# Recurrence units of a delta-rule mixer: two 64x64 chunks per tile on the partition halves, eight tap buffers

## The reference, cut to what matters

```
def _wkv7(r, decay, k, v, a_vec, b_vec):
    def step(S, inp):
        r_t, w_t, k_t, v_t, a_t, b_t = inp
        sa = jnp.einsum("bhvk,bhk->bhv", S, a_t)
        S = S * w_t[:, :, None, :] + sa[..., None] * b_t[:, :, None, :] + v_t[..., None] * k_t[:, :, None, :]
        y = jnp.einsum("bhvk,bhk->bhv", S, r_t)
        return S, y
...
    y = _wkv7(r_h, decay.reshape(B, T, H, N), k_h, v_h, -kk, kk * a_h)
...
    c = u[..., :D_CONV] * jax.nn.sigmoid(u[..., D_CONV:])
    c = _causal_dwconv(c, cconv_w, cconv_b)
    c = jax.nn.silu(_layer_norm(c, cln_g, cln_b))
```

## Time and profile before

| what | value |
|---|---|
| median of 3 executions | 1712.69 us (1710.89 to 1716.49) |
| the profiled execution | 1717.92 us |
| its span in the profile | 1716.1 us |
| TensorE busy over the span | 1651.0 us, 96% |
| VectorE, ScalarE, GpSimd busy | 1008.8, 734.9, 958.2 us |
| mean granted TensorE clock | 0.981 of full speed |

### The profile page before, as it was taken

How to read it: one execution, slowest core, us unless ns; L and a number is a source line. 1 busy time by engine, 2 the same in 40 slices (tenths; PEclk the granted TensorE clock), 3 DMA queues, 4 the chain that set the end, 5 groups by cost and what they waited for, 6 DMA issues and landing times.

```text
span 1716.1 us, 26361 instructions
## 1 busy us (share of the span) xinstructions
PE 1651.0 (96%) x10600; PEld 1353.4 (79%) x10600; DVE 1008.8 (59%) x1271; ACT 734.9 (43%) x1250; POOL 958.2 (56%) x758
## 2 busy tenths in 40 slices
PE   8999999899999999998999999999989999999887
PEld 7677999867888888887886777767877888888775
DVE  4699566574755553004446667665665666666565
ACT  4553787433322221005325565654144444444562
POOL 3454799783999999995462203217535444444062
PEclk9999999999999999999999999999989999999998
DMA  5221000542222224332111000003131111111211
GB/s 198 74 78 70 2 1 1 201 147 99 95 92 92 92 96 172 121 135 78 71 50 50 1 25 25 0 1 130 53 151 49 50 50 50 50 50 50 99 50 49
DMA packets 18872, 126.40 MB, mean 74 GB/s; under 512 B 2096, under 2 KB 2352, under 8 KB 4304
## 3 DMA queue, kind: packets, MB, share of 16 engines
q1 hardware_dynamic: 18624, 124.41, 20.0%
q10 hardware_dynamic: 144, 0.52, 0.1%
HBM read 122.83 MB, written 2.10 MB: 73 GB/s over the span
## 4 chain that ended last, share of the span: by engine, by line
PE 59%; issue 16%; POOL 11%; DVE 8%; ACT 5%; DMA 0%; POOLq 0%; ACTq 0%; DVEq 0%; SPq 0%
POOL w_hi L654 8%; PE banks L1293 5%; PE banks L905 4%; PE banks L1272 4%; POOL w_lo L645 4%; PE banks L1450 4%; PE banks L1453 3%; PE banks L1451 3%; PE banks L1155 3%; PE banks L1160 3%; PE banks L1156 3%; PE banks L1505 2%; PE banks L757 2%; PE banks L758 2%; PE banks L759 2%
## 5 line engine op out<-in xcount | busy, mean ns | idle before, releaser
L654 POOL TENSOR_TENSOR w_hi<-raw,der 128x512 fp32r<-128x512 f32 x296 | 332.7, 1134 | 428.4 <-PE banks L1453 187.3
L645 POOL TENSOR_TENSOR w_lo<-raw,w_hi 128x512 fp32r<-128x512 f32 x336 | 479.4, 1439 | 67.1 <-ACT w_hi L1596 67.1
L757 PE MATMUL banks<-h_hi,w_hi 128*128 128x512 f32 x464 | 184.3, 397 | 0.3 <-DVEq L2271 0.3
L758 PE MATMUL banks<-h_lo,w_hi 128*128 128x512 f32 x464 | 180.7, 389 | 0.0
L759 PE MATMUL banks<-h_hi,w_lo 128*128 128x512 f32 x464 | 180.6, 389 | 0.0
L1450 PE MATMUL banks<-h_hi,w_hi 128*128 128x512 f32 (+1 forms) x384 | 147.1, 383 | 0.1
L1451 PE MATMUL banks<-h_lo,w_hi 128*128 128x512 f32 (+1 forms) x384 | 132.1, 359 | 0.0
L2111 ACT ACTIVATE dP<-banks,der 128x768 f32<-128x768 f32 x64 | 57.7, 902 | 161.0 <-DVE der L2920 161.0
L704 POOL TENSOR_TENSOR Of<-Of,Ls 128x768 f32<-128x768 f32 x8 | 14.7, 1833 | 186.7 <-DVE Ls L2722 186.7
L1453 PE MATMUL banks<-h_hi,w_lo 128*128 128x512 f32 (+1 forms) x384 | 117.1, 359 | 0.0
L757 PEld LDWEIGHTS banks<-h_hi,w_hi 128*128 128x128 f32 x464 | 87.1, 188 | 25.6 <-issue 7.5
(11 more groups left out here) (507 smaller groups left out, 4089.1 us busy)
## 6 DMA issues: line engine op xcount, KB each, us to landing
raw<-in_stream SPq DMA_DIRECT2D x84, 1024.0 KB, 4.8
ada_raw<-in_ada_w SPq DMA_DIRECT2D x18, 1024.0 KB, 7.0
raw<-in_ada_w SPq DMA_DIRECT2D x4, 1024.0 KB, 4.8
xT<-in_x_t SPq DMA_DIRECT2D x2, 1024.0 KB, 6.1
xT<-in_x_t SPq DMA_DIRECT2D x1, 2048.0 KB, 8.2
ada_end<-in_ada_w SPq DMA_DIRECT2D x2, 1024.0 KB, 6.0
out_t<-z SPq DMA_DIRECT2D x8, 256.0 KB, 2.1
ctxT<-in_ctx_t SPq DMA_DIRECT2D x1, 1024.0 KB, 7.0
```

Of the source, the lines that this page charges most:

```text
L645: return pool.tensor_tensor(lo[:, h, part(i), :], raw_tiles(half)[:, part(i), :], hi[:, h, part(i), :], ALU.subtract)
L654: pool.tensor_tensor(hi[:, h, part(i), :], raw_tiles(half)[:, part(i), :], one, ALU.mult).then_inc(hi_done, 1)
L757: pe.matmul(banks[b][:, :], hi, tile(rhs_hi, k), start=(at_k == 0), stop=False)
L758: pe.matmul(banks[b][:, :], hi, tile(rhs_lo, k), start=False, stop=False)
```

## The change

A unit's 128-token tile becomes two chunks of 64, on the two halves of the partitions. Every tile Di, DiT, Lt, Gt, Mt, RKt and RBt is 128 x 4 x 64 in place of 128 x 4 x 128, and each 128x128 product becomes two products of 64x64 by 64x64, whose places in the PE array alternate. A step of one head is eight matmuls in place of four. The copies, masks, placements and transposes are over 256 columns in place of 512. Mt has a tile of its own, DiT has two in turn (c even or odd), and the orders of PE, ACT and DVE are written out by hand: the next pair's LT and identity come ahead of this pair's Q5, W and U. Three PSUM banks serve a head: one for G (and W), one for LT and P, one for all the rest, so that MT, RB, RK, MV, Y0, Q5 and U of a head wait for one another's readers. Y0's copy and W's scaling are one instruction for both heads. The scaling of eR stands by itself (`eR`, once a pair). The taps stay on ScalarE and GpSimd with eight buffers in place of four, and all stand behind G1 to G5 and U (5, 4, 4, 4, 3, 4 in each pair); none stand behind the identity, MV or Y0.

```
-    tap_out = [glu_s[:, 0, :], glu_s[:, 1, :]] + [reg(f"tap_out{i}", [P, T], 141 + 2 * i)[:, :] for i in range(2)]
+    tap_out = [glu_s[:, 0, :], glu_s[:, 1, :]] + [reg(f"tap_out{i}", [P, T], kb)[:, :] for i, kb in enumerate((141, 143, 46))] + \
+        [at(f"tap_out{3 + i}", [P, T], F32, tmp_at + 2 * i * KB)[:, :] for i in range(3)]
...
+    PE_ORDER, ACT_ORDER, DVE_ORDER = [(0, "LT")], [(0, "ID"), (0, "LT")], [(0, "DT0", 0), (0, "D0", 0), (0, "DT0", 1), (0, "D0", 1)]
+    for c in range(CT):
+        last = c == CT - 1
+        PE_ORDER += [(c, s) for s in ("MT", "G1", "RB", "P1", "RK", "G2", "P2", "MV", "G3", "P3", "Y0", "G4", "P4", "G5")]
+        PE_ORDER += ([] if last else [(c + 1, "LT")]) + [(c, s) for s in ("Q5", "W", "U")]
+        ACT_ORDER += [(c, s) for s in ("G1", "G2", "MV", "G3", "Y0", "G4")] + ([] if last else [(c + 1, "ID")])
+        ACT_ORDER += [(c, "G5")] + ([] if last else [(c + 1, "LT")]) + [(c, "U")]
+        DVE_ORDER += [(c, "MT", 0), (c, "MT", 1), (c, "P1", 0), (c, "T1", 0), (c, "P1", 1), (c, "T1", 1), (c, "RB", 0), (c, "RB", 1),
+                      (c, "P2", 0), (c, "T2", 0), (c, "P2", 1), (c, "T2", 1), (c, "RK", 0), (c, "RK", 1),
...
+    PROD_BANK, BACK_BANK, MIX_BANK = (0, 1), (2, 3), (4, 5)
...
+            def by_chunk(b, lhs, rhs):
+                for tt in range(4):
+                    for r in HEAD:
+                        mm = pe.matmul(b[r, CHUNK * tt:CHUNK * tt + CHUNK], lhs[r, tt, :], rhs[r, tt, :], start=True, stop=True)
+                mm.then_inc(u_pe[e], 1)
...
         def tap(i):
             t, j = ADDED[i]
-            if i >= 4:
-                act.wait_ge(conv_done, i - 3)
...
+            if i >= len(tap_out):
+                act.wait_ge(conv_done, i - len(tap_out) + 1)
...
-        TAPS_BEHIND = {"DIT": 5, "MV": 1, "Y0": 1, "G1": 3, "G2": 3, "G3": 3, "G4": 3, "G5": 3, "U": 2}
+        TAPS_BEHIND = {"G1": 5, "G2": 4, "G3": 4, "G4": 4, "G5": 3, "U": 4}
```

More of the change, by code:

```diff
@@ new lines, in by_chunk, with to_features @@
+            def by_chunk(b, lhs, rhs):
+                for tt in range(4):
+                    for r in HEAD:
+                        mm = pe.matmul(b[r, CHUNK * tt:CHUNK * tt + CHUNK], lhs[r, tt, :], rhs[r, tt, :], start=True, stop=True)
+                mm.then_inc(u_pe[e], 1)
+            def to_features(out, lhs, rhs):
+                for tt in range(4):
+                    for half, r in enumerate(HEAD):
+                        mm = pe.matmul(banks[out[half]][rows, CHUNK * tt:CHUNK * tt + CHUNK], lhs[r, tt, cols], rhs[r, tt, :], start=True, stop=True)
+                mm.then_inc(u_pe[e], 1)
@@ L919, in _ @@
+        for c, step in PE_ORDER:
+            for e in range(2):
+                unit(c, e, step)
         pe.wait_ge(silu_c, 1)
@@ L1728, in _ @@
-        next_tap = 0
-        for c in range(CT):
-            for step in ACT_STEPS:
-                for e in range(2):
-                    unit(c, e, step)
-                n_taps = TAPS_BEHIND.get(step, 0)
-                for i in range(next_tap, next_tap + n_taps):
-                    tap(i)
-                next_tap += n_taps
+                out, src = U[:, :, 64 * h:64 * h + 64], banks[MIX_BANK[e]]
+            act.activation(out, src[:, 0:256].rearrange("p (a b) -> p a b", a=4), ACT.Copy).then_inc(u_act[e], 1)
@@ new lines, in _ @@
+        TAPS_BEHIND = {"G1": 5, "G2": 4, "G3": 4, "G4": 4, "G5": 3, "U": 4}
+        next_tap = 0
+        act.wait_ge(block_done, N_IN)
+        for c, step in ACT_ORDER:
+            if step == "Y0":
+                first_y(c)
+            else:
+                for e in range(2):
+                    if step == "ID":
+                        identity(c, e)
+                    else:
+                        unit(c, e, step)
+            for i in range(next_tap, next_tap + TAPS_BEHIND.get(step, 0)):
+                tap(i)
+            next_tap += TAPS_BEHIND.get(step, 0)
@@ L2419, in unit @@
                 dve.wait_ge(u_pe[e], pe_at(c, step))
-                placed(*((Di[e], bank(1), n) if step[0] == "P" else (DiT[e], bank(2), 6 + n)))
-        for c in range(CT):
-            for step in DVE_STEPS:
-                for e in range(2):
-                    unit(c, e, step)
+                placed(*((Di[e], bank(BACK_BANK), n) if step[0] == "P" else (T_now, bank(MIX_BANK), 6 + n)))
+        for c, step, e in DVE_ORDER:
+            unit(c, e, step)
+        chain.wait()
         chain.link(dve.memset(der[:, ROOT:ROOT + 4], 0.0))
```

266 lines of the change are left out of this document (127 added, 139 removed).

## The result

The changed kernel takes **1726.99 us** (median of 10, 1720.00 to 1730.33) against 1713.89 of the kernel before on the same chip (median of 10): a ratio of 1.0072, 95% interval 1.0057 to 1.0086. It is 0.7% slower. 1705.1 was forecast, with 1699 to 1716 as the range. The profiled execution's span is 1728.5 us for 1716.1.

The account below looks back on a forecast made before the run. PE was taken to set the units' pace, GpSimd's adds close behind and next to bound. Earlier end of adds -6.6 and chunk chain -1.0 make -7.6 us: median 1712.69 becomes 1705.1, range 1699 to 1716.

Parts of the forecast that it names:

- the cost of VectorE: Units: VectorE's small operations, eR and W take 13.5 us a pair, below the adds.
- case (a): Units: GpSimd's tap adds set the pace, 30.15 us a pair; kernel at 1701 to 1709 us; chance 0.70.
- The adds' end: Units: last GpSimd tap add ends at 303.2 against 309.77, -6.6 us, with a first add at 182.6.
- the chain: Chunk chain behind the adds: between +3.0 and -5.1 us, taken as -1.0.
- The price of a record: PE in the units: a 64x64 product's record costs 0.032 us at full clock, 0.0575 at half.
- Rival (c): Units: each PE record costs 0.0575 us throughout, 39.6 us a pair; kernel slower at 1743 us; chance 0.08.
- The loop of a pair: Units: PE's work of 18.5 us plus 6.5 without work makes 25 us a pair at full clock.
- rival (b): Units: the unit loop sets the pace through clock falls and larger bubbles; kernel at 1708.5 to 1715.3 us; chance 0.14.
- Rival (e): Units: a 64x64 pair costs as much as a 128x128 product, 32 us a pair; chance within that of rival (b).
- Rival (d): Chunk chain: issue stretches vanish, half clock is short, start at its lower bound; kernel at 1699 to 1702 us; chance 0.08.
- The cold restart: Chunk chain: starts at half clock after 11 idle us; 3.5 us of it lose 1.5, 6.9 lose 3.0.
- GpSimd idle in the middle of the stage: Units: sign that the forecast is wrong, pointing to rival (b) or Rival (c) by the granted clock.

Follow-up runs that it names:

- e2: Changed kernel with the decay operand of eR's scaling read from a PSUM bank: 1709.75 us, 0.9948 of the kernel before.
- e10: Changed kernel with the decay in PSUM and 20 taps of channel block 3 moved to VectorE: 1695.41 us, 0.9886 of the kernel before.
- e8: e2 with the wait for the adds and conv_sums one chunk later (n = 2) in the chunk chain: 0.9949 of the kernel before.
- e9: e8 with the first two taps taken ahead to the first LT: 0.9937 of the kernel before.
- e13: Changed kernel, eR's scaling behind a long-met wait in pairs 0, 1, 3 and written to another tile in pair 2: 1730.13 us, a single time.
- e6: e2 with 28 added VectorE products of 8 columns, both operands in SBUF, seven a pair: 1729.82 us, a single time.
- e11: e2 with 28 added VectorE products of 512 columns, both operands in SBUF, at the places of e6: 1726.75 us, a single time.
- e3: Changed kernel with four tap buffers in place of eight: 1.0045 of the kernel before.

## Why the prediction was wrong, point by point

**The step that failed** is the cost of VectorE: "VectorE has 28 small ones, 11.8, and eR and W, each put at two small ones, 1.7: 13.5. Both lie below the adds." For all of these but eR it held (0.45, 0.43, 0.42, 0.68 us each). eR was put at the price of its size; it cost 38.7 us in all, 36 more than four times 0.65. The sum then took for granted that VectorE has more than half of the time free, and never asked which of its instructions can run beside a GpSimd add. The earlier trace rows gave a hint, the two adds beside eR at 206.69 with 2.94 us against 2.52. The forecast read this as a cost to GpSimd (0.42 us, inside the 120.60) and not as a sign that the two take turns. That they do is in the kernel before already. VectorE, then GpSimd around it:

```profile
207.64 0.86 DVE L2392 TENSOR_TENSOR eR<-eR,der 128x512 f32<-128x512 f32 x1
```

```profile
207.91 1.71 POOL L676 TENSOR_TENSOR cacc<-glu_s,cacc 128x512 f32<-128x512 f32 x1
210.93 1.27 POOL L676 TENSOR_TENSOR cacc<-tap_out,cacc 128x512 f32<-128x512 f32 x1 [1.30 <-ACT tap_out L1694]
```

eR stands at 207.64 with an add running and one filled buffer behind it. It is let in at the end of the running add, and the next add takes 1.71 us. The gap of 1.30 us comes only after both. So eR did not need a gap in the kernel before, in any of its four pairs, and what changed so that it is held in three of four is not shown. What is shown is the price of a hold: it lasts until GpSimd has nothing to do, and "GpSimd without idle" is what the forecast wanted.

The Trainium skill has the rule (SBUF — State Buffer, Who interferes with whom): a VectorE instruction with two inputs in SBUF contends with a GpSimd instruction that reads SBUF, by an exclusive lock, and one with a single SBUF input doesn't (outside of modes that take two ports). The traces agree on who contends: eR does, W and e2's eR don't. By the same section the one that issues first has the ports for its whole instruction; the other would then wait for one add, an estimated 1.3 us at most by the adds' length here. For 53 of the 56 probes, the four eR of the kernel before and the first of the changed kernel the traces agree: where there was a wait, it ended with the running add. For the others they differ: eR stood for 10 to 13.9 us, with seven to ten adds started after it.

**The mechanism behind it was right, where it could work.** The likeliest case (a), the adds set the pace, is what e2 shows once eR is out of the way: first add 182.72 (182.6), last 301.59 (303.2), the units' end on PE at 289.2 (288), `conv_sums` 8.7 us earlier than before, and 337.39 against 345.90 for the output projection, -8.5 us for a forecast of -7.6. The adds' end moved by -8.2 where -6.6 was forecast (adds of 1.230 us in place of 1.256 give -2.5, idle +0.8, the start +0.1); `conv_sums` stands closer behind them, -0.5; the chain gave +0.2 where -1.0 was taken. That the total of e2 comes so near the forecast is in part luck, as the misses of -1.6 and -0.5 make up for the +1.2 of the chain. In time e2 is 0.52% faster; the forecast was 0.44%.

**The price of a record** held: 32 in 0.96 us at full clock, 0.030 us, and 1.73 us, 0.054, at the lower level (forecast 0.032 and 0.0575). Rival (c), half clock or issue throughout, is excluded by this. One reading beside it was wrong and touches no term of the sum. The prediction set the 62 ns per matmul of the Trainium skill (TensorE: Matmul & The Clock Gate, Back-to-back issue gap) against the 32 records of a step. But the profile records each matmul twice, so a step has 16 matmuls, and 16 times 62 ns is an estimated 0.99 us. That is close to the 1.03 us of the row: the trace doesn't speak against that figure, and the 2.0 us a step and the +15 us of rival (c) that were worked out from it fall. **The loop of a pair** was put at 25 us and is at most 23.5 (e10), so rival (b) had the wrong place: the pace of the changed kernel, 37.0 and 36.6 us from one eR to the next (261.77 - 224.73, 298.34 - 261.77), is neither the hand-overs' nor the clock's. The clock did fall behind gaps of 1 to 2 us as (b) had it (0.57 in 186.50 to 190.50), and that cost nothing beyond the adds: e2 has it too, at 0.87 over the units. Rival (e), that a pair of 64x64 products costs as much as a 128x128, fell with the record's price. Rival (d), a chain that gives back more, did not come: 37.4 us, and 35.7 in e2, for 35.6 before.

**The cold restart** was right: some 6.9 us at the lower level, of 3.5 to 6.9. The chain is 37.4 us, within the bound of 38.5 that was set for it. Of the signs of being wrong, "GpSimd idle in the middle of the stage" is the one that came, but neither (b) nor (c) was behind it.

**What no rival had** is a wait between VectorE and GpSimd. The list of rivals went through PE, ScalarE, SyncE, the clock and the chain, and left out the pair of engines that share something other than a semaphore.

## What to carry to other kernels

Before a change makes GpSimd busy without gaps, list the VectorE instructions in that stretch that read two tiles in SBUF, and move one operand of each into PSUM (or the instruction out of the stretch); the size of the instruction doesn't matter. When an operation grows by ten times at the same shape, compare its start and end with the neighbour engine's: an end right behind the neighbour going idle (0.55 us here) says what to test first. And a price taken from a trace (eR, 0.86 to 0.90 us four times out of four) holds for that order of events; for an operation that takes turns with another engine it is worth an entry of its own in the sum, with what a turn passed over would cost. e8 and e9, built when the cause was known, met the same hold in an add of 8 columns that they had moved.

## What the hardware did that was not expected

A VectorE product with both operands in SBUF can be passed over by GpSimd's adds again and again: ten adds in 13.91 us at 128x512, and six in 7.48 us at 128x8, until GpSimd has nothing to do. GpSimd's splits of weights do it as well: ten instructions passed an add of 128x8 in 12.15 us (e8), and the same add took 7.00 us in e13. It isn't always so: 25 of the 28 small probes of e6 and all 28 wide ones of e11 got in at the latest at the end of the add that was running, at a cost of 0.45 us to GpSimd for each wide one. The same instruction at the same place was held in three pairs of four, in three kernels (after, e3, e13). What decides is open; length of the operation, depth of the buffers, a wait ahead and the place of the result were tried, and none of them decides by itself. With one operand in PSUM the scaling takes 0.65 us beside adds that go on at 1.230 us each.
